# A ring of eight slots instead of ten for gathered expert rows, and the query weights of two heads kept in place

## What is computed

```python
h = h + merged @ w_out
h = h + _peer(_rmsnorm(h, norm2_g), peer_w_q, peer_sub_keys, peer_u, peer_v)
...
q = (xb @ w_q).reshape(tb, PEER_HEADS, 2, PEER_HALF)
s = jnp.einsum('thpc,pkc->thpk', q, sub_keys)
...
experts = i1 * PEER_NKEYS + i2
gate = jax.nn.softmax(cv, axis=-1)
u = u_tab[experts]
act = jax.nn.gelu(jnp.einsum('thkd,td->thk', u, xb), approximate=False)
w = gate * act
return jnp.einsum('thk,thkd->td', w, v_tab[experts])
```

## Time and profile before

| | us |
|---|---|
| median of three runs | 1943.35 |
| profiled execution | 1947.41 |
| its span, first to last instruction | 1945.6 |

### The profile page before, as it was taken

One profiled execution on the slowest core, in us unless ns is written; L12 is line 12 of the kernel. 1 busy time (PEld: TensorE's weight loads), 2 busy tenths in 40 slices (PEclk: granted clock), 3 DMA queues, 4 the chain that ended last, 5 costly groups with the idle time before them and its releaser, 6 DMA issues.

```text
span 1945.6 us, 17733 instructions
## 1 busy us (share of the span) xinstructions
PE 1674.4 (86%) x5411; PEld 999.5 (51%) x5411; DVE 1388.4 (71%) x3407; ACT 521.7 (27%) x1203; POOL 663.9 (34%) x605
## 2 busy tenths in 40 slices
PE   8999999999888999998868999877777777787876
PEld 7888987887555555554434555323333212333332
DVE  5998684227788777777787778776777776777754
ACT  3121142113333433332222223332222122321221
POOL 0020030002434343333434344444444453445441
PEclk9999999999999999999979999998999898989898
DMA  5452465548999999999989999999999999999995
GB/s 209 141 87 98 154 146 164 176 150 339 418 400 412 419 418 418 418 419 401 419 349 413 419 420 414 421 422 410 414 419 413 412 416 419 408 414 415 421 412 245
DMA packets 112687, 675.14 MB, mean 347 GB/s; under 512 B 12784, under 2 KB 15296, under 8 KB 42576
## 3 DMA queue, kind: packets, MB, share of 16 engines
q0 software_dynamic: 80816, 577.23, 73.0%
q1 hardware_dynamic: 31216, 95.87, 14.3%
q10 hardware_dynamic: 560, 0.92, 0.2%
HBM read 665.79 MB, written 6.21 MB: 345 GB/s over the span
## 4 chain that ended last, share of the span: by engine, by line
PE 46%; DMA 36%; issue 8%; DVE 6%; POOL 2%; ACT 2%; ACTq 0%; DVEq 0%; POOLq 0%
DMA upper<-in_peer_uv,upper 20%; PE pair L1157 19%; DMA lower<-in_peer_uv,upper 16%; PE pair L667 7%; PE pair L678 6%; PE pair L1024 4%; DVE upper L2080 2%; PE pair L781 2%; ACT upper L1550 1%; PE pair L972 1%; POOL upper L643 1%; DVE lower L2080 1%; POOL lower L643 1%; PE pair L793 1%; PE pair L712 1%
## 5 line engine op out<-in xcount | busy, mean ns | idle before, releaser
L1157 PE MATMUL pair<-upper 128*128 128x512 f32 (+1 forms) x1144 | 570.4, 641 | 152.6 <-ACT upper L1550 152.3
L643 POOL DMA_INDIRECT upper<-in_peer_uv,upper x324 | 369.2, 1139 | 500.6 <-PE pair L1157 437.4
L1157 PE MATMUL pair<-lower,upper 128*128 128x512 f32 (+1 forms) x772 | 382.1, 637 | 93.7 <-ACT upper L1550 93.6
L1157 PEld LDWEIGHTS pair<-upper 128*128 128x128 f32 (+1 forms) x1144 | 218.5, 198 | 434.0 <-issue 276.0
L643 POOL DMA_INDIRECT lower<-in_peer_uv,upper x220 | 255.2, 1160 | 483.0 <-PE pair L1157 305.0
L2080 DVE CUSTOM_DVE_ANT_0 upper<-upper 128x1024 f32<-128x1024 f32 x172 | 210.7, 1225 | 122.4 <-DMA upper<-in_peer_uv,upper 122.1
L1157 PEld LDWEIGHTS pair<-lower,upper 128*128 128x128 f32 (+1 forms) x772 | 148.0, 198 | 283.5 <-issue 185.5
L2080 DVE CUSTOM_DVE_ANT_0 upper<-upper,lower 128x1024 f32<-128x1024 f32 x152 | 185.8, 1222 | 87.6 <-DMA upper<-in_peer_uv,upper 86.7
L1550 ACT ACTIVATE upper<-upper 128x128 f32<-128x128 f32 (+1 forms) x479 | 159.9, 386 | 308.3 <-DVE upper L2096 308.1
L2080 DVE CUSTOM_DVE_ANT_0 lower<-lower,upper 128x1024 f32<-128x1024 f32 x116 | 142.1, 1225 | 85.5 <-DMA lower<-in_peer_uv,upper 85.5
L1024 PE MATMUL pair<-lower 128*128 128x288 f32 x704 | 194.0, 413 | 2.6 <-ACT upper L1420 2.6
(11 more groups left out here) (420 smaller groups left out, 1760.6 us busy)
## 6 DMA issues: line engine op xcount, KB each, us to landing
lower<-in_w_in SPq DMA_DIRECT2D x64, 512.0 KB, 7.0
lower<-in_peer_q SPq DMA_DIRECT2D x32, 512.0 KB, 7.9
lower<-in_proj SPq DMA_DIRECT2D x48, 256.0 KB, 7.1
lower<-in_w_out SPq DMA_DIRECT2D x16, 512.0 KB, 6.0
upper<-in_peer_uv,upper POOLq DMA_INDIRECT x324, 11.8
upper<-in_cache_k SPq DMA_DIRECT2D x8, 512.0 KB, 4.5
upper<-in_cache_v SPq DMA_DIRECT2D x8, 512.0 KB, 3.7
lower<-in_peer_uv,upper POOLq DMA_INDIRECT x220, 11.8
```

Source lines behind the costliest of these rows:

```text
L643: pool.indirect_dma_start(row(g), None, a["peer_uv"], bass.IndirectOffsetOnAxis(ap=idx[:, n % 8, j:j + 1], axis=0)).then_inc(row_in[g % RI ...
L1157: mm = pe.matmul(pairs[n % 2][0:rows, h, :], diag[:, (nth - 1) % DIAGS, 0:rows], row(g)[:, D + h * 512:D + (h + 1) * 512], start=(j == min ...
```

## The change

The ring of gathered rows gets eight slots. In the room of slots 8 and 9, `kept_w`, lie the four blocks of query weights of heads 0 and 1 (`KEPT`). SP loads them once, behind the first group's inputs and ahead of its branch products, after a wait for the layer norm's seventh step (`lnx_ok`), the last that reads what lay there. Both groups read them there. The loads of these heads leave the ring of four (`BANK_LOADS`), and the loads behind them move up in it.

```diff
--- before.py
+++ after.py
@@ -49,7 +49,7 @@
 TWO_PI_HI = 6.28125
 TWO_PI_LO = 2 * PI - TWO_PI_HI
 NEG = -3.0e38
-RING = 10
+RING = 8
 DIAGS = 8
 LAG = 2
 GROUP = 4
@@ -123,7 +123,8 @@
 BANK = {n: (i % 4, i // 4) for i, n in enumerate(_names)}
 
 
-BANK_LOADS = ["Aq0.0", "Aq0.1"] + [n for n in _names if n[0] in "gpwq" or n[:2] == "Aq"]
+KEPT = {f"{_a}{_h}.{_b}": 2 * _h + _b for _a in ("Aq", "q") for _h in range(2) for _b in range(2)}
+BANK_LOADS = [n for n in _names if (n[0] in "gpwq" or n[:2] == "Aq") and n not in KEPT]
 BANK_LOAD = {n: (i % 4, i // 4) for i, n in enumerate(BANK_LOADS)}
 
 
@@ -302,6 +303,7 @@
         h2sq = at(30976, KD, FIRST)
         xbT = at(44728, KD, FIRST)
         late_w = at(0, 4, 1024)
+        kept_w = at(33024, 4, 1024)
         qbuf = at(4096, 2, 2, RQ)
         gsg_b = at(22912, 2, 3, REST)
         merged_b = at(44728, KD, REST)
@@ -400,6 +402,7 @@
         bank_full = [sem(f"bank_full{i}") for i in range(4)]
         bank_free = [sem(f"bank_free{i}") for i in range(4)]
         late_in = [sem(f"late_w_in{i}") for i in range(4)]
+        kept_in = [sem(f"kept_w_in{i}") for i in range(4)]
         x2b_in, mergeb_ok, h2sqb_ok, h2rb_ok, xbTb_ok = (sem(n) for n in (
             "x2b_in", "mergeb_ok", "h2sqb_ok", "h2rb_ok", "xbTb_ok"))
 
@@ -519,6 +522,9 @@
                 sp.dma_start(v, vm.rearrange("p a b -> p (a b)")[:, 896 * m:896 + P * m]).then_inc(kv_copied, 16)
             sp.dma_start(h2T, a["x_t"][:, :, 0:FIRST]).then_inc(x2_in, 16)
             sp.dma_start(h2T_b, a["x_t"][:, :, FIRST:]).then_inc(x2b_in, 16)
+            sp.wait_ge(lnx_ok, 2 * HALF - 1)
+            for i in range(4):
+                sp.dma_start(kept_w[:, i, :], a["peer_q"][i]).then_inc(kept_in[i], 16)
             for n in PRODUCTS:
                 q, b = int(n[1]), int(n[3])
                 load(n, a["proj"][b][q], HALF)
@@ -530,15 +536,14 @@
                 if m < 4:
                     before = JOB_NUMBER[f"o{m + 2}"]
                     sp.wait_ge(full[before % 4], before // 4 + 1)
-                elif m < 6:
-                    sp.wait_ge(first_q, m - 3)
                 else:
                     bank_filled(sp, BANK_LOADS[m - 4])
                 sp.dma_start(late_w[:, m % 4, 0:k * P], src).then_inc(late_in[m % 4], 16)
 
             for h in range(PH):
                 for b in range(2):
-                    late_load(f"Aq{h}.{b}", a["peer_q"][2 * h + b])
+                    if f"Aq{h}.{b}" not in KEPT:
+                        late_load(f"Aq{h}.{b}", a["peer_q"][2 * h + b])
             for q in range(KD):
                 for b in range(3):
                     late_load(f"g{q}.{b}", a["w_in"][16 + 8 * b + q])
@@ -549,7 +554,8 @@
             sp.dma_start(gf, a["final_g"].partition_broadcast(P)).then_inc(gf_in, 16)
             for h in range(PH):
                 for b in range(2):
-                    late_load(f"q{h}.{b}", a["peer_q"][2 * h + b])
+                    if f"q{h}.{b}" not in KEPT:
+                        late_load(f"q{h}.{b}", a["peer_q"][2 * h + b])
             for n, t in enumerate((0, 1, 2, 4, 3)):
                 sp.wait_ge(yt_ok, n + 1)
                 rows = P if t < TILES else NB * NT
@@ -917,6 +923,10 @@
                     pe.wait_ge(cact_ok, HALF)
                 first(n, (zg, cact, qT)[b], HALF)
             def late_weights(name):
+                if name in KEPT:
+                    s = KEPT[name]
+                    pe.wait_ge(kept_in[s], 16)
+                    return kept_w[:, s, :].rearrange("p (k m) -> p k m", m=P)
                 s, n = BANK_LOAD[name]
                 pe.wait_ge(late_in[s], 16 * (n + 1))
                 return late_w[:, s, :].rearrange("p (k m) -> p k m", m=P)
```

## The result

The changed kernel takes 2187.41 us (median of four runs, 2179.23 to 2194.3) against 1943.78 us before on the same chip: 1.125 times as long, 95% interval 1.122 to 1.128. It is 244 us slower; 73 us were forecast, and the range ended at 2070. The profiled execution took 2179.23 us, 8 us under that median, and its span is 2177.4; so the trace can place 231.8 us of the loss.

The account below looks back on a forecast made before the run. DMA was taken as the bound. Last stretch 58, trunk-side stretches 10 and pauses 10, less 5 for loads, gave 73 us on the 1943.35 us median: 2016 us, range 1968 to 2070.

Parts of the forecast that it names:

- The cycle: Time per group of four gathered rows: about 11 us over the last 272 rows, 11.9 us where second-group weights travel.
- The step that failed: Next group's first landing to gather issue (4.65 or 6.39 us) plus landing alone (5.77) exceeds eight slots' 9.96 us.
- the prediction's rule: Gathered rows land 2.49 us apart; a gather with no other in flight lands 5.77 us after its issue.
- The last stretch: Last 272 gathered rows, 692.02 us before: DMA runs dry once per group, bounds 52 and 67 us, 58 taken.
- The two stretches beside the weights: 36 groups: nothing lost at full clock, up to 0.86 us each at low; bounds 0 and 31, 10 taken.
- Where the weights travel: Second group's weights travel beside gathers: DMA needs 11.89 us per group, more than 10.42, so nothing is lost.
- Two pauses: POOL stands still at the gathers' start and ahead of 1019.22: two rows fewer in flight, 5.0 us each, 10 us.
- Loads: Query weights of heads 0 and 1 read once: four 512 KB loads less, late in the gathers, saving 5.0 us.
- The move of the loads: Four query loads moved from about 406 to about 339 us on SP: costed at nothing, at most 5.0 us.
- That the landing is shorter with others in flight: Gathers land in 4.74 us, so only the 28 slow groups lose: +27 us, 1970 us; chance 18%.
- That the clock falls in every group: TensorE's longer pauses bring the low clock, cycle 12.16 us in all groups: +173 us, 2116 us; chance 15%.
- That the queue never runs dry: Two rows still transferring cover each new gather, leaving only the loads' saving of 5 us: 1938 us; chance 5%.

Follow-up runs that it names:

- eight slots alone: Kernel before the change with an eight-slot ring and nothing else, all 32 query loads kept: 2182.9 us, ratio 1.122.
- nine slots: Kernel before the change with a nine-slot ring and nothing else: 2002.74 us, ratio 1.030.
- eight slots, early weights: Changed kernel, with VectorE making a group's weights ahead of the dot of the next group's first row instead of behind it: 2047.01 us, ratio 1.054.
- nine slots, early weights: Kernel before the change with a nine-slot ring and a group's weights made ahead of the next group's first dot: 1947.36 us, ratio 1.0016.
- limit of four: Kernel before the change, ten slots, with POOL issuing gather g only when gather g-4 has landed: 1942.92 us, ratio 0.999.
- limit of three: Kernel before the change, ten slots, with POOL issuing gather g only when gather g-3 has landed: 2079.34 us, ratio 1.074.
- limit of two: Kernel before the change, ten slots, with POOL issuing gather g only when gather g-2 has landed: 2408.67 us, ratio 1.239.

## Why the prediction was wrong

**The direction held, and the mechanism in its outline.** The ring became too short, the DMA share of the last stretch fell under 1.0, the first dot of a group waits longest (the 2.10, 1.58 and 2.89 us above; over the last stretch 1.88 us on average against 1.16, 1.19 and 0.68 of the other three), the median landing is within the 6 to 9 us named. The cycle is 12.28 us where about 11 was forecast, and where the weights travel it is 307.05 / 24 = 12.79 instead of the 11.9 that were to stay. Both came out worse, and the landings show the same thing in both.

**The step that failed** is "It needs 4.65 + 5.77 = 10.42 us at the full clock and 6.39 + 5.77 = 12.16 us at the low one": that a gather needs its turn and a *lone* landing, after which the three rows behind it "are not late again". The forecast cycle is the mean turn of 5.16 us that its mix gives plus 5.77, 10.9 us. Measured are 5.66 + 6.62. So 0.50 us a group are a larger share of long turns (48 of 67 instead of 28 of 69), and 0.85 are a landing that is not lone: behind short turns, where two rows were still under way, it took 7.82.

What the landing depends on can be read from each gather. By the prediction's rule a row lands 2.49 us behind the one before it, or 5.77 us after its own issue if that is later. I compared the last 288 landings of several kernels with this, by how many others were in flight at the issue:

| kernel | 3 or more others | 2 others | 1 other |
|---|---|---|---|
| before | 0.05 us late (288) | - | - |
| changed | 0.04 (83) | **0.56** (141) | 0.18 (64) |
| eight slots alone | 0.02 (84) | **0.57** (143) | 0.15 (61) |
| nine slots | 0.03 (204) | **0.53** (82) | 0.02 (2) |
| eight slots, early weights | 0.00 (174) | **0.64** (93) | 0.46 (21) |
| nine slots, early weights | 0.04 (274) | 0.07 (14) | - |
| limit of four | 0.04 (288) | - | - |
| limit of three | - | **0.38** (288) | - |
| limit of two | - | - | 0.60 (288) |

With three or more others the rule is right. With one other it is about right too: the landing is bound by its own 5.77, and counted from the end of the issue, which sometimes takes longer, these rows are late by 0.02, 0.01, 0.02, -0.09 and -0.1 us. With two it fails by some half a us on average, in all kernels but the one with nine slots and early weights.

The number is not all there is to it. What these rows hang on more closely is the time that is left, at the end of the issue, until the row ahead lands. The rule takes the later of two times, which meet where 5.77 - 0.94 - 2.49 = 2.34 us are left. In the changed kernel, eight slots, nine slots and eight with early weights together, gathers with two others in flight are 0.89 us late where 2 to 4 us are left (258), and 0.10 where 4.5 or more are left (126); with one other and 2 to 4 us left, 39 gathers are 0.55 late. So the rule holds where one of its times is clearly the later, and mostly fails where they lie close. That is not all of it either: with nine slots and early weights 11 gathers had two others and 2 to 4 us left, and are 0.08 us late. With the limit of three 3.7 us are left on average; 0.86 more, from an issue of 0.94 us, would make that 4.5, an estimate that no run tests. The group shown has such a gather: at 1948.91 two others are under way, the later of them landed at 1952.46 (VectorE took it up at 1953.09), so 1954.95 was due; it came at 1956.67, 1.7 us late. The issue ended at 1949.90, so 2.56 us were left. That is one of the worse ones.

And in a closed ring each late landing is the next turn's start. So the saving of a short turn is lost again in a longer landing, which is why the clock made no difference, and why the sum was too small in every stretch.

**Where the late time sits.** DMA share times interval is the busy time of the engines for a row: 1.01 x 2.54 = 2.57 us before, 0.91 x 3.07 = 2.79 in the changed kernel, 0.97 x 2.86 = 2.77 with three in flight. Of the 0.53 us that a row costs more, 0.22 are thus engines that are busy for longer with the same bytes, and 0.31 are engines that stand idle. The queues on the page say the same of the whole run; the gathers' queue, the same packets, before:

```profile
q0 software_dynamic: 80816, 577.23, 73.0%
```

and changed:

```profile
q0 software_dynamic: 80816, 577.23, 69.8%
```

That is 0.730 x 1945.6 = 1420 us of packets before and 0.698 x 2177.4 = 1520 after. Why an engine's packets take longer when little is queued is not shown by these runs.

**Term by term.** The last stretch, "took 58": 143.5 us. The two stretches beside the weights, "took 10", with bounds of 0 and 31: 16.2 + 42.9 = 59.1, of which the pause at 1019 may be a part. Where the weights travel, "nothing is lost there": 21.6 us. The reason given, that the DMA needs 11.89 us for a group there, more than 10.42, again set a lone landing against a busy queue. In that stretch before, all 96 gathers were issued with three or more others in flight and landed 2.97 us apart. With the change it is 27, which come 2.89 us behind the landing ahead; 63 with two others come 3.27 behind it, and 6 with one 3.81. Two pauses, 10 us: at row 16 the changed kernel is 508.78 - 505.34 = 3.4 us behind, so the first was not larger than its 5; the second can't be told apart. Loads, "-5": nothing that shows with eight slots, where the DMA engines have time to spare in most groups; 3.0 us for two of them where the queue is full. The move of the loads, at nothing: right. SP issues them at 339.49 and the first product load 3.9 us later than before, TensorE starts its first product at 356.72 instead of 356.24.

```profile
339.49 3.69 SPq L527 DMA_DIRECT2D upper<-in_peer_q  x4
343.21 20.93 SPq L482 DMA_DIRECT2D lower<-in_proj  x11
356.72 1.89 PE L684 MATMUL pair<-upper,lower 128*128 128x256 f32 x8
```

**The rivals.** That the landing is shorter with others in flight (1970 us) was wrong in its sign: behind the turns it was 6.62 us on average, and 5.77 alone. The estimate of 4.4 us from the Trainium skill, "DMA: Bandwidth & Descriptors", section "Anatomy of one DMA — SWDGE (gpsimd) path", was weighed for it; no gather here landed under 5.3 us. That the clock falls in every group (2116 us) came true for most, 48 of 67 turns, but with the clock given back up to the level of before the time stayed. That the queue never runs dry (1938 us) relied on two rows still under way to cover a gather. With two the time that is left is mostly too short for that.

The landings of the earlier trace rows could have been a warning: with landings of 8.0 to 15.0 us at 2.49 to 2.54 us each, none of its last 288 gathers was issued with fewer than three others in flight, so that trace held nothing on what two others do. The range should have had a bound for that, and took only the lone landing, from which two to three in flight looked like enough.

## What to carry to other kernels

Before a ring is shortened, divide the landing by the interval of landings: that is the number in flight, and the trace of before vouches for the rate at that number alone. Here gathers of 1 MB had the full 416 GB/s with some four in flight, itself counted: a mean of 3.8 was enough, 3.5 was not. A lone landing divided by the interval says 2.3 and is too low. To see which gathers come late, take for each the time from the end of its issue to the landing ahead of it: here 4.5 us or more were enough with two others in flight as well. Where a slot is wanted for something else, first shorten the time from landing to release (here one line moved on VectorE), then take the slot.

## What the runs showed of the hardware

- Rate of the gathers by number in flight in the last stretch: 1.9 gives 311 GB/s and 2.9 gives 369 (both with the longer issue), 2.6 gives 344, 3.4 gives 377, 3.5 gives 396; 3.8 to 4.9 (five kernels, the 3.8 with the longer issue) give 415 to 417.
- An issue on POOL takes 0.94 us by itself, but 1.80 us at the median where it starts just after a dot on VectorE has started, as it does with a limit of three:

```profile
1500.21 1.23 DVE L2082 CUSTOM_DVE_ANT_0 upper<-upper 128x1024 f32<-128x1024 f32 x1
1500.44 1.80 POOL L645 DMA_INDIRECT lower<-in_peer_uv,upper  x1 [1.66 <-DMA upper<-in_peer_uv,upper]
```

  The dot ends at 1501.44, the issue 0.80 us later, as if it had begun only then. The Trainium skill, "GPSIMD Engine Reference", section "1. Specifications", has GpSimd's SBUF interfaces shared with VectorE, in contention where its instruction reads two SBUF inputs, which a dot does. The traces agree: in each of the twelve kernels, among the last 288 gathers, an issue that starts within a dot ends 0.81 us behind that dot's end at the median, whichever part of the dot was left, and one that starts outside a dot takes 0.94 us. With four in flight the longer issue cost nothing.
- TensorE's granted clock in the last stretch was 0.92 before and 0.85 with the change, where TensorE stood idle for 395 us ahead of the rows' matmuls instead of 246. With other matmuls in such pauses it was 0.93, and no time that shows came back: 2184.54 against 2187.41 us.
